# The head of a two-layer diffusion backbone in another order: halves of the channels, shift and scale first

## The reference, cut to what matters

```python
silu_c = jax.nn.silu(c)
m = jnp.split((silu_c @ w_mod[i] + b_mod[i])[:, None, :], N_MOD, axis=-1)   # nine vectors of 1024
h = h + 0.5 * m[2] * swiglu(modulate(rms_norm(h), m[0], m[1]), w_ff_in[i, 0], w_ff_out[i, 0])
# modulate(h, shift, scale) = h * (1 + scale) + shift
# swiglu: g, u = split(h @ w_in);  (silu(g) * u) @ w_out
```

## Time and profile before

| | us |
|---|---|
| median of 3 runs | 1856.83 (1856.17 to 1857.86) |
| the profiled execution, whole | 1856.64 |
| its span, from the first to the last instruction | 1854.9 |
| TensorE busy | 1803.0 (97%) |
| VectorE busy | 1197.2 (65%) |
| ScalarE busy | 619.6 (33%) |
| GpSimd busy | 170.1 (9%) |

### The profile page before, as it was taken

One profiled execution on the slowest core, in us unless ns is written; L12 is line 12 of the kernel. 1 busy time (PEld: TensorE's weight loads), 2 busy tenths in 40 slices (PEclk: granted clock), 3 DMA queues, 4 the chain that ended last, 5 costly groups with the idle time before them and its releaser, 6 DMA issues.

```text
span 1854.9 us, 22066 instructions
## 1 busy us (share of the span) xinstructions
PE 1803.0 (97%) x8604; PEld 1485.3 (80%) x8604; DVE 1197.2 (65%) x1541; ACT 619.6 (33%) x796; POOL 170.1 (9%) x148
## 2 busy tenths in 40 slices
PE   5899999998999999999999999999999999999999
PEld 2688888888798888888988888889764898888888
DVE  6866767567767675676776766547798555444454
ACT  2532222235342222222432222225766542222221
POOL 0000000002110000000200000002995200000000
PEclk8999999998999999999999999999999999999999
DMA  8853634431436344363253453421120322413201
GB/s 293 272 187 115 219 119 163 176 113 47 136 114 218 123 161 179 113 217 123 69 200 140 144 195 113 136 68 46 46 92 24 116 89 69 136 68 112 91 23 69
DMA packets 160395, 238.10 MB, mean 128 GB/s; under 512 B 3805, under 2 KB 110509, under 8 KB 160204
## 3 DMA queue, kind: packets, MB, share of 16 engines
q1 hardware_dynamic: 160016, 236.99, 36.9%
q10 hardware_dynamic: 316, 0.23, 0.0%
HBM read 235.11 MB, written 2.10 MB: 128 GB/s over the span
## 4 chain that ended last, share of the span: by engine, by line
PE 85%; DVE 5%; POOL 4%; ACT 3%; DMA 1%; issue 1%; SPq 0%; POOLq 0%; DVEq 0%; ACTq 0%
PE bank L1670 16%; PE bank L1677 15%; PE bank L1672 15%; PE bank L1545 10%; PE bank L1547 10%; PE bank L1546 10%; POOL tmp_c L628 3%; PE bank L1927 2%; PE bank L1615 1%; DVE mod_acc L1025 1%; PE bank L1617 1%; PE bank L1619 1%; DVE w_lo L992 1%; DMA raw_pair<-in_w_mod 1%; POOL sq_sum L593 1%
## 5 line engine op out<-in xcount | busy, mean ns | idle before, releaser
L1670 PE MATMUL bank<-a_hi,w_hi 128*128 128x512 f32 x1408 | 552.6, 392 | 6.2 <-ACT a_hi L686 4.7
L1672 PE MATMUL bank<-a_hi,w_lo 128*128 128x512 f32 x1408 | 549.3, 390 | 0.0
L1677 PE MATMUL bank<-a_lo,w_hi 128*128 128x512 f32 x1408 | 434.8, 390 | 1.7 <-DVE a_lo L1100 1.6
L1670 PEld LDWEIGHTS bank<-a_hi,w_hi 128*128 128x128 f32 x1408 | 265.3, 188 | 63.7 <-issue 6.3
L1218 DVE SCALAR_TENSOR_TENSOR h<-bank,half_gate,h 128x512 f32<-128x512 f32 x320 | 233.5, 746 | 122.3 <-PE bank L1547 121.7
L1677 PEld LDWEIGHTS bank<-a_lo,w_hi 128*128 128x128 f32 x1408 | 264.8, 188 | 57.7 <-DVE a_lo L1100 2.7
L1672 PEld LDWEIGHTS bank<-a_hi,w_lo 128*128 128x128 f32 x1408 | 265.4, 188 | 56.3 <-issue 1.4
L1545 PE MATMUL bank<-p_hi,w_hi 128*128 128x512 f32 (+1 forms) x768 | 287.6, 375 | 1.1 <-DVE h L1225 0.6
L1547 PE MATMUL bank<-p_lo,w_hi 128*128 128x512 f32 (+1 forms) x768 | 285.9, 372 | 0.0
L1546 PE MATMUL bank<-p_hi,w_lo 128*128 128x512 f32 (+1 forms) x768 | 285.7, 372 | 0.0
L992 DVE TENSOR_TENSOR w_lo<-raw_pair,w_hi 128x2048 fp32r<-128x2048 f32 x102 | 235.4, 2308 | 51.8 <-ACT w_hi L800 47.9
(11 more groups left out here) (197 smaller groups left out, 1851.6 us busy)
## 6 DMA issues: line engine op xcount, KB each, us to landing
raw_pair<-in_w_ff_in SPq DMA_DIRECT2D x88, 1024.0 KB, 7.4
raw_mod<-in_w_mod SPq DMA_DIRECT2D x66, 1024.0 KB, 8.3
raw_down<-in_w_ff_out SPq DMA_DIRECT2D x44, 1024.0 KB, 8.6
raw_pair<-in_conv_w_in SPq DMA_DIRECT2D x8, 1024.0 KB, 6.6
raw_pair<-in_w_mod SPq DMA_DIRECT2D x6, 1024.0 KB, 15.2
...
```

What stands on the lines that cost most here:

```text
L1670: pe.matmul(ps[banks + s][:], tile_hi, a_hi[:, k], start=k == 0, stop=False, skip_group_check=True)
L1672: pe.matmul(ps[banks + s][:], tile_lo, a_hi[:, k], start=False, stop=False, skip_group_check=True)
L1677: ins = pe.matmul(ps[banks + s][:], w_hi[b][:, s * KD + k], a_lo[:, k], start=False, stop=k == KD - 1, skip_group_check=True)
```

## The change

x goes into the first weight pair's buffer and unit 2 and unit 1 into `raw_mod`, so all weight pairs change to the other buffer. The squares of x are added by GpSimd. Units 0 and 2 (shift and scale of channels 0 to 511) are finished first, and chunks 0 to 3 are normalised, modulated and multiplied with both tiles of the first weight pair (`head_up`); units 1 and 3 are finished among and behind these, and chunks 4 to 7 follow. The first weight pair is loaded ahead of unit 1. The counts of the semaphore for finished columns change with the number of column steps.

```diff
-    PAIR = {FFA: 0, FNET: NI, FFB: NI + 3, FFC: 2 * NI + 3, CONV: 3 * NI + 3, FFD: 3 * NI + 9}
+    PAIR = {FFA: 1, FNET: NI + 1, FFB: NI + 4, FFC: 2 * NI + 4, CONV: 3 * NI + 4, FFD: 3 * NI + 10}
...
-        x_rows = raw_mod[:].rearrange("p a b n -> p (a b n)").rearrange("p (t d) -> p t d", t=TC)
+        x_rows = raw_pair[0][:].rearrange("p a b n -> p (a b n)").rearrange("p (t d) -> p t d", t=TC)
...
-        head_rows = [slot_rows[1], slot_rows[1], slot_rows[0], raw_mod[:].rearrange("p a b n -> p (a b) n")]
+        mod_slot = raw_mod[:].rearrange("p a b n -> p (a b) n")
+        head_rows = [slot_rows[1], mod_slot, mod_slot, slot_rows[0]]
...
-        HEAD_BANK = {2: 2, 3: 3}
+        HEAD_BANK = {2: 2, 3: 4}
+        HEAD_T_BANK = [0, 6]
...
             sp.wait_ge(s_mod_mac, KD)
+            ff_pair(0, 0, PAIR[FFA])
+
+            sp.wait_ge(s_head_sum, 1)
             head_load(1)
 
-            sp.wait_ge(s_head_sum, 1)
-            ff_pair(0, 0, 0)
-
             sp.wait_ge(s_head_sum, 2)
+            ff_pair(0, 1, PAIR[FFA] + 1)
+
+            sp.wait_ge(s_mod_mac, 2 * KD)
             for half, src in enumerate(mod_unit(0, HEAD * MU)):
                 sp.dma_start(raw_mod[:, half], src).then_inc(s_mod_in[half], 16)
-
-            sp.wait_ge(s_mod_mac, 2 * KD)
-            ff_pair(0, 1, 1)
...
+            for o in range(1, KD):
+                pool.wait_ge(s_sq, o + 1)
+                if o == 1:
+                    pool.tensor_tensor(sq_sum[:], tmp_a[:, 0], tmp_a[:, 1], ALU.add).then_inc(s_sq_sum, 1)
+                else:
+
+                    pool.wait_ge(s_sq_sum, o - 1)
+                    pool.tensor_tensor(sq_sum[:], sq_sum[:], tmp_a[:, o % 2], ALU.add).then_inc(s_sq_sum, 1)
...
-            def modulated(n, func, scale, bias, after=()):
+            def modulated(n, func, scale, bias, ks=range(KD)):
 
                 q = n // 5
-                for k in range(KD):
+                for k in ks:
...
             squares(0, h, [(KD - 1, lambda: mod_hi(0))])
+
+            def head_chunks(ks):
+                modulated(0, ACT.Identity, mod[:, 0, KD:2 * KD], mod[:, 0, 0:KD], ks)
+
+            act.wait_ge(s_mod, 2)
+            head_chunks(range(1))
+            pair_hi(FIRST[FFA][0], PAIR[FFA], 0)
+            head_chunks(range(1, 3))
+            pair_hi(FIRST[FFA][1], PAIR[FFA], 1)
+            head_chunks(range(3, 4))
             mod_hi(1)
-            pair_hi(FIRST[FFA][0], 0, 0)
-
-            act.wait_ge(s_mod, 2)
-            modulated(0, ACT.Identity, mod[:, 0, KD:2 * KD], mod[:, 0, 0:KD],
-                      [(4, lambda: pair_hi(FIRST[FFA][1], 0, 1))])
+            act.wait_ge(s_mod, 4)
+            head_chunks(range(4, KD))
             feed_forward(0, (FIRST[FNET][0], PAIR[FNET]))
...
 
+                dve.wait_ge(s_mod_t, call + 2)
+                row_range_columns(MOD_T_BANK[call], *MOD_CALLS[call])
+
+            def head_columns(call):
+
                 dve.wait_ge(s_mod_t, call + 1)
-                row_range_columns(call, *MOD_CALLS[call])
-                if call == 0:
-                    row_range_columns(call, ROWS - 2, ROWS, 2)
-
-            def row_range_columns(call, row0, row1, unit0):
+                row_range_columns(HEAD_T_BANK[call], call, call + 1, call)
+                row_range_columns(HEAD_T_BANK[call], HEAD_ROW + 2 + call, HEAD_ROW + 3 + call, 2 + call)
...
-            def normed(n, src, after=()):
+            def normed(n, src, ks=range(KD), after=()):
...
                 dve.tensor_copy(h[:, d], ps[d % 4][:]).then_inc(s_h, 1)
-                if d >= 1:
-                    square_add(0, d - 1)
-            square_add(0, KD - 1)
...
             mod_lo(0)
-            mod_row(0)
-            token_rstd(0)
-            head_row(2)
-            head_mac(1)
-            mod_lo(1)
-            head_row(3)
-            dve.wait_ge(s_head_row, 2)
-            mod_row(1)
...
             dve.wait_ge(s_vec, NV + 2)
-            pair_lo(FIRST[FFA][0], 0, 0)
-            mod_columns(0)
-            normed(0, h, [(4, lambda: pair_lo(FIRST[FFA][1], 0, 1))])
+            token_rstd(0)
+            mod_row(0)
+            head_row(2)
+            head_columns(0)
+            normed(0, h, range(4), [(0, lambda: pair_lo(FIRST[FFA][0], PAIR[FFA], 0)),
+                                    (2, lambda: pair_lo(FIRST[FFA][1], PAIR[FFA], 1))])
+            head_mac(1)
+            mod_lo(1)
+            head_row(3)
+            dve.wait_ge(s_head_row, 2)
+            mod_row(1)
+            head_columns(1)
+            normed(0, h, range(4, KD))
             feed_forward(0, (FIRST[FNET][0], PAIR[FNET]))
...
-            def head_sum(unit):
+            def head_half(unit, half):
+
+                pe.wait_ge(s_head_in[2 * unit + half], 16)
+                for k in range(4 * half, 4 * half + 4):
+                    ins = pe.matmul(ps[HEAD_BANK[unit]][0:ROWS, :], silu_c[:, k:k + 1].to_broadcast([P, ROWS]),
+                                    head_rows[unit][:, k], start=k == 0, stop=k == KD - 1, skip_group_check=True)
+                if half == 1:
+                    ins.then_inc(s_head_sum, 1)
+
+            def head_transpose(call):
+
+                pe.wait_ge(s_mod_row, call + 1)
+                pe.wait_ge(s_head_row, call + 1)
+                for j in range(UC):
+                    ins = pe.transpose(ps[HEAD_T_BANK[call]][:, j * ROWS:(j + 1) * ROWS],
+                                       mod_rows[:, j * P:(j + 1) * P], ident[0:ROWS, 0:ROWS])
+                ins.then_inc(s_mod_t, 1)
+
+            def head_up():
 
                 for half in range(2):
-                    pe.wait_ge(s_head_in[2 * unit + half], 16)
-                    for k in range(4 * half, 4 * half + 4):
-                        ins = pe.matmul(ps[HEAD_BANK[unit]][0:ROWS, :], silu_c[:, k:k + 1].to_broadcast([P, ROWS]),
-                                        head_rows[unit][:, k], start=k == 0, stop=k == KD - 1)
-                ins.then_inc(s_head_sum, 1)
+                    for ch, (b, use) in enumerate(UP[0]):
+                        if half == 0:
+                            pe.wait_ge(s_w[b], use + 1)
+                        for k in range(4 * half, 4 * half + 4):
+                            pe.wait_ge(s_a_hi, k + 1)
+                            for s in range(2):
+                                bank = ps[2 * ch + s]
+                                pe.matmul(bank[:], w_hi[b][:, s * KD + k], a_hi[:, k], start=k == 0, stop=False,
+                                          skip_group_check=True)
+                                pe.matmul(bank[:], w_lo[b][:, s * KD + k], a_hi[:, k], start=False, stop=False,
+                                          skip_group_check=True)
+                            pe.wait_ge(s_a, k + 1)
+                            for s in range(2):
+                                ins = pe.matmul(ps[2 * ch + s][:], w_hi[b][:, s * KD + k], a_lo[:, k], start=False,
+                                                stop=k == KD - 1, skip_group_check=True)
+                            if k == KD - 1:
+                                ins.then_inc(s_gu, 1)
+                            if ch == 1 and k == 2:
+                                mod_sum(1)
+                            if ch == 1 and k == 3:
+                                head_transpose(1)
...
                 if f == 0:
-                    up(f, 0, 0, True)
-                    up(f, 0, 1, False)
+                    head_up()
...
             pe.wait_ge(s_silu_c, 1)
             pe.wait_ge(s_h, KD)
-            head_sum(2)
-            mod_sum(0)
-            token_sums(0)
...
             ins.then_inc(s_vec_t, 1)
+            head_half(2, 0)
+            token_sums(0)
+            mod_sum(0)
+            head_half(2, 1)
             spread_rstd(0)
-            head_sum(3)
-
-            pe.wait_ge(s_mod_row, 1)
-            mod_sum(1)
-            pe.wait_ge(s_head_row, 2)
-            mod_transpose(0)
+            head_half(3, 0)
+            head_transpose(0)
+            head_half(3, 1)
             feed_forward(0, 0)
```

More of the change, by code:

```diff
@@ L133, in hybrid_backbone @@
     HN = [1, 2, 3, 4, 6]
-    NORM_MOD = [4, 4, 6, 6, 7]
+    NORM_MOD = [6, 6, 8, 8, 9]
     NORM_FF = {1: 0, 3: 1, 4: 2}
@@ L160, in hybrid_backbone @@
     SEQ = [(0, 1), (1, 1), (0, 0), (1, 0)]
-    GATE_MOD = [3, 5, 6, 7]
+    GATE_MOD = [5, 7, 8, 9]
     ADDS = KD - 1
@@ L647, in pair_hi @@
                 b = unit[0]
-                act.wait_ge(s_pair_in[pair % 2], 32 * (pair // 2 + 1))
+                act.wait_ge(s_pair_in[pair % 2], 32 * ((pair + 1) // 2))
                 act.activation(w_hi[b][:], raw_pair[pair % 2][:, :, j, :], ACT.Copy).then_inc(s_w_hi[b], 1)
@@ L692, in modulated @@
                                    scale=scale[:, k:k + 1]).then_inc(s_a_full, 1)
-                    for at, work in after:
-                        if at == k:
-                            work()
             def half_square(n, hf, o):
@@ L796, in next_hi @@
```

(20 more changed lines are left out.)

1 line of the change is left out of this document (added).

## The result

The kernel after takes **1862.35 us** (median of 7 runs, 1860.55 to 1864.64) against 1856.71 (1854.49 to 1857.97, 7 runs) for the kernel before in the same session: ratio 1.0032, 95% interval 1.0023 to 1.0041. It is 0.3% slower; 1862.2 was forecast. The profiled execution took 1863.93, its span 1862.1.

The account below looks back on a forecast made before the run. The prediction took VectorE's chain in the head, before TensorE's steady part, as the bound: +4.3 us for VectorE's lateness and +1.1 for the clock make +5.4, giving 1862.2 us, range 1858.0 to 1865.5.

Parts of the forecast that it names:

- What to follow: Head: when VectorE reaches the accumulate at 64.46 us sets the end, not when TensorE starts its products at 49.80.
- Step 1: Head up to the first normalised chunk: VectorE starts chunk 0 at 38.6 us against 48.07, 9.5 us earlier.
- Step 2: Chunks 0 to 3 with both weight splits among them, ScalarE and VectorE alternating: 13.1 us, to 51.7.
- Step 3: Unit 1's sum, row updates and columns, moved behind chunk 3 onto VectorE's chain: 10.0 us, to 61.7.
- Step 4: Chunks 4 to 7 on VectorE: 7.1 us, to 68.8; TensorE finishes its first products near 75.0 and waits for VectorE.
- +4.3: VectorE's lateness at the accumulate of 64.46, now 68.8: -9.5 + 13.1 + 10.0 + 7.1 against 16.4 before.
- Step 5: TensorE's low clock after pauses: chunk 3's products 0 to +1.4, the head's last stretch 0 to +1.2; +1.1 for both.
- Edits at nothing: Squares on GpSimd (6 us cover), earlier unit 0 accumulate, first weight pair there by 38, buffer swap: all cost nothing.
- Contention: VectorE's unit 0 accumulates beside GpSimd's additions: +0.9 us for each of four, unit 0 ending near 27.5; price 0.
- B: Rival, faster: the start of TensorE's products (44.9 instead of 49.8) decides, not VectorE; 1851 to 1853 us; chance 0.08.
- C: Rival, no difference: set-up transposes near 16.5 keep TensorE's clock up, -1.75, later pauses cost nothing; 1859.4 us; chance 0.17.
- D: Rival, worse: contention beyond its cover (+2.5) or the first weight pair landing late; 1865 to 1868 us; chance 0.13.

Follow-up runs that it names:

- e10: The kernel after with TensorE's transposes of the first two rows ahead of unit 3's first half instead of behind it: 1858.51 us, ratio 1.0009 to the kernel before.
- e3: The kernel after with each of unit 1's last seven accumulate steps on VectorE issued twice: 1869.49 us, ratio 1.0067 to the kernel before.
- e1: The kernel after with the seven additions of squares back on VectorE instead of GpSimd: 1862.71 us, ratio 1.0032 to the kernel before.
- e2: The kernel after with unit 1's last seven accumulate steps over 8 of 512 columns: 1859.02 us, ratio 1.0012 to the kernel before.
- e5: The kernel after with unit 1 summed by TensorE behind unit 3 instead of by VectorE: 1855.45 us, ratio 0.9990 to the kernel before.
- e11: The kernel after with unit 1 on TensorE, six more matmuls, and the first transposes ahead of unit 3's first half: 1852.88 us, ratio 0.9981 to before.
- e7: The kernel after with unit 1 on TensorE and six more matmuls in TensorE's idle time: 1853.25 us, ratio 0.9980 to the kernel before.
- e4: The kernel before with only the seven additions of squares moved to GpSimd: 1856.44 us, ratio 0.9999 to the kernel before.
- e6: The kernel after with six more matmuls in TensorE's idle time before unit 2 lands: 1859.94 us, ratio 1.0017 to the kernel before.

## Why the prediction was right, step by step

- *What to follow.* Right. The accumulate of 64.46 is 5.3 us late, the transposes of 90.07 5.3 us, the medians 5.6. The first product is 4.1 us early and that bought nothing.
- *Step 1*, chunk 0 at 38.6: 39.27. The term for unit 2's first half was 5.25 and measured 5.88 here, since the low clock lasted longer. It is a matter of the execution and not of the change: it varies between executions of kernels that are alike up to there: 4.93 in e10, 5.08 in e3, 5.19 in e1, 5.68 in e2, 6.31 in e5.
- *Step 2*, 13.1 us to 51.7: from 39.27 to 52.48, 13.2. ScalarE and VectorE do alternate, as laid out.
- *Step 3*, 10.0 us: from 52.48 to 62.55, 10.1. This is the step that decides, and e3 and e5 show it: a block 4.65 us longer is paid in full, and with the block off VectorE 7.3 us are gained (6.3 by the mark).
- *Step 4*, 7.1 us: 7.2. So +4.3 became +5.3, 0.7 of the added us in step 1 and the rest tenths of the other steps. TensorE's end of the first products was put at 75.0, and lay near 77.3, since the low clock came back in them (0.64 at 65 to 66 us) and the first product was 0.8 us later than reckoned; nobody waited for it, VectorE was later still.
- *Step 5*, the clock, +1.1: this term was mis-sized. In the profiled execution both its parts are 0: chunk 3's products ran at full clock, and the last stretch took 13.0 us from the transposes to the sum (95.38 to 108.38) as before (90.07 to 103.09). The statement behind it, that each such pause has the low clock behind it, is wrong: the pauses of 1.66, 2.06 and 1.70 us before 59.98, 79.39 and 92.61 did not, those of 3.10, 1.83 and 2.15 before 45.74, 64.19 and 95.38 did. The length alone does not decide, for 1.83 did and 2.06 did not. In e1, where the pause before the sum is 2.52 us, it does happen (0.65 at 60 to 61, 0.50 at 61 to 62), VectorE waits 1.77 instead of 0.93 us for the transposes, and chunk 4 starts at 62.52 although unit 1's steps started 0.9 us earlier than in the kernel after. So the first part exists, in some executions, at 0.8 us (0.95 in e10), and so does the second: 14.3 us in e2 and 14.0 in e10 instead of 13.0. That the total came out at 1862.2 for 1862.35 is luck: 1.1 us were charged for the clock and not paid, and 1.0 us were missing from steps 1 to 4. The mechanism and the size of the moved block were right.
- *Edits at nothing.* Right. GpSimd's last addition ends at 23.29 (cover to 28.97), unit 0's low part at 27.58 (wanted at 29.89), and the first pair is converted at 41.47 without a wait for its transfer. It has not much room: in e11, 3.5 us earlier, VectorE waits 2.80 us for the conversion, where e7 waits 1.11, since the pair landed only at 37.8 (by 38 was reckoned).
- *Contention.* The price of 0 on the end is borne out by e1 and e4. The size was right too: the four steps that met additions took 1.64 us (one 1.56) instead of 0.75, the +0.9 that the prediction took from 1635 against 745. It left out that the unit's first operation, with one SBUF operand, would meet an addition as well: 1.26 us instead of 0.48. Unit 0 ended at 26.20 all the same and not at 27.5, since it began early, at 15.88; without additions beside it, it would have ended near 21.9 (15.88 + 0.5 + 5.5) and not at 23.6. The rule of the Trainium skill ("SBUF — State Buffer", "Who interferes with whom") has the one engine blocked for the whole of the other's instruction. The rows agree in that the two take turns: an addition ends at 19.94, a step at 20.49, the next addition at 21.62, the next step at 22.17. They differ in the size: one of each takes 1.67 us, where the whole durations alone add up to 0.75 + 1.27 = 2.0, so some 0.35 us of the pair do overlap.
- *Rivals.* B fell: the first product started 4.1 us earlier and the end came 5.6 later, so the products' start does not decide. C's mechanism did not occur in the kernel after: the set-up transposes stood at 18.88 and not at 16.5, since they waited for a transfer (`raw_down`), behind a pause of 3.88 us and at a clock of 0.50, and 2.5 us of pause followed; with more matmuls there (e6) it does occur, and is worth 2.2 to 2.8 us. D did not occur.

The last 0.2 us of the difference, 5.6 against 5.4, are below what these runs resolve.
